# A gated delta rule's triangular inverse: level masks moved from GpSimd ahead of a product to VectorE behind it, and VectorE's dense work reordered around the transposes

## The reference, cut to what matters

```python
kk = jnp.einsum('bhnid,bhnjd->bhnij', k, k)
A = jnp.where(strict, beta[..., :, None] * kk * decay, 0.0)
eye = jnp.eye(C, dtype=F32)
rhs = jnp.concatenate([v * beta[..., None], k * (beta * jnp.exp(gc))[..., None]], axis=-1)
sol = lax.linalg.triangular_solve(A + eye, rhs, left_side=True, lower=True, unit_diagonal=True)
u = sol[..., :dv]
w = sol[..., dv:]
```

## Time and profile before

| | |
|---|---|
| median of three runs | 2222.99 us (2217.79 to 2225.85) |
| the profiled execution: its time / its span | 2220.19 us / 2218.4 us |
| mean granted TensorE clock | 0.987 of full speed |
| busy: TensorE matmul / weight loads | 2136.5 us (96%) / 1758.6 us (79%) |
| busy: VectorE / ScalarE / GpSimd | 1151.9 us (52%) / 762.5 us (34%) / 202.2 us (9%) |
| the four pairs' stretch, 1510 to 1810 us: TensorE / weight loads / VectorE / GpSimd busy | 277.98 / 231.02 / 204.56 / 67.29 us of 300 |
| GpSimd's masks L1580 | 24, in 1510.8 to 1761.5 us |

### The profile page before, as it was taken

One profiled execution on the slowest core, in us unless ns is written; L12 is line 12 of the kernel. 1 busy time (PEld: TensorE's weight loads), 2 busy tenths in 40 slices (PEclk: granted clock), 3 DMA queues, 4 the chain that ended last, 5 costly groups with the idle time before them and its releaser, 6 DMA issues. The chain is left out here.

```text
span 2218.4 us, 33573 instructions
## 1 busy us (share of the span) xinstructions
PE 2136.5 (96%) x13592; PEld 1758.6 (79%) x13592; DVE 1151.9 (52%) x1444; ACT 762.5 (34%) x1047; POOL 202.2 (9%) x137
## 2 busy tenths in 40 slices
PE   7999999997988999999999999998999999999998
PEld 6888888774977888888888888877887778888886
DVE  5444434568557544443444443377667665444422
ACT  4322223245233323322322322253554453322221
POOL 2000011000412000001000001103112210000011
PEclk9999999998999999999999999999999999999999
DMA  4322321320012233332233332221111122333321
GB/s 177 95 95 95 119 96 51 119 66 1 4 42 83 90 101 95 98 112 93 76 96 99 98 116 92 77 87 40 39 43 46 50 66 96 95 95 97 121 91 51
DMA packets 48271, 182.95 MB, mean 82 GB/s; under 512 B 6320, under 2 KB 6576, under 8 KB 48048
## 3 DMA queue, kind: packets, MB, share of 16 engines
q1 hardware_dynamic: 48176, 181.58, 25.6%
HBM read 179.46 MB, written 2.10 MB: 82 GB/s over the span
## 5 line engine op out<-in xcount | busy, mean ns | idle before, releaser
L546 PE MATMUL banks<-H,WS 128*128 128x512 f32 x1840 | 733.0, 398 | 18.4 <-DVE H L1695 8.9
L547 PE MATMUL banks<-H,WS 128*128 128x512 f32 x1840 | 720.7, 392 | 0.0
L548 PE MATMUL banks<-H,WS 128*128 128x512 f32 x1840 | 720.6, 392 | 0.0
L1123 ACT ACTIVATE WS<-RAW 128x1024 fp32r<-128x1024 f32 (+1 forms) x310 | 349.1, 1126 | 995.5 <-PE banks L548 981.9
L1616 DVE TENSOR_TENSOR WS<-RAW,WS 128x1024 fp32r<-128x1024 f32 (+1 forms) x310 | 408.7, 1319 | 217.9 <-ACT WS L1123 217.7
L546 PEld LDWEIGHTS banks<-H,WS 128*128 128x128 f32 x1840 | 347.6, 189 | 97.0 <-DVE WS L1616 11.2
L548 PEld LDWEIGHTS banks<-H,WS 128*128 128x128 f32 x1840 | 347.8, 189 | 73.8
L547 PEld LDWEIGHTS banks<-H,WS 128*128 128x128 f32 x1840 | 347.8, 189 | 71.0 <-issue 1.9
L546 PE MATMUL banks<-A,WS 128*128 128x512 f32 x704 | 273.9, 389 | 0.0
L547 PE MATMUL banks<-A,WS 128*128 128x512 f32 x704 | 273.9, 389 | 0.0
L548 PE MATMUL banks<-A,WS 128*128 128x512 f32 x704 | 273.9, 389 | 0.0
(11 more groups left out here) (352 smaller groups left out, 1777.7 us busy)
## 6 DMA issues: line engine op xcount, KB each, us to landing
RAW<-in_w_gate SPq DMA_DIRECT2D x88, 512.0 KB, 3.6
RAW<-in_w_up SPq DMA_DIRECT2D x88, 512.0 KB, 3.6
RAW<-in_w_down SPq DMA_DIRECT2D x64, 704.0 KB, 4.0
RAW<-in_c_in SPq DMA_DIRECT2D x32, 512.0 KB, 3.6
RAW<-in_ab_in SPq DMA_DIRECT2D x22, 512.0 KB, 3.6
RAW<-in_ab_out SPq DMA_DIRECT2D x8, 512.0 KB, 4.2
RAW<-in_c_out SPq DMA_DIRECT2D x8, 512.0 KB, 3.7
X<-in_x SPq DMA_DIRECT2D x4, 512.0 KB, 6.7
```

Of the source, the lines that this page charges most:

```text
L546: pe.matmul(bank[:, :], WS[:, 0, s, cols], src[0][:, r, :], start=first and j == 0, stop=False)
L547: pe.matmul(bank[:, :], WS[:, 0, s, cols], src[1][:, r, :], start=False, stop=False)
L548: mm = pe.matmul(bank[:, :], WS[:, 1, s, cols], src[0][:, r, :], start=False, stop=last and j == len(rows) - 1)
L1123: act.activation(WS[:, 0, c % SPLIT, 0:cols], RAW[:, c % RING, 0:cols], ACT.Copy).then_inc(hi_ready, 1)
```

## The change

- The constants. The 128-wide pair masks go. New are six masks of 64 columns, `minus1` to `minus32`: -1 on the diagonal and on the entries that belong to the level, 0 elsewhere (for all levels but the first the mask is transposed, since it is laid on the product).
- GpSimd makes C_TM once in a pair, in two steps: the strict triangle of C_TTH, then minus the identity. The masks per level are gone: two instructions instead of six in each pair. For p > 0 the first step waits until the previous pair's last u product has read C_TM.
- VectorE makes C_XT as C_TM times `minus1`, for which it now waits for GpSimd's second step, and C_IU in each level as the product in the bank times the level's mask. The product is now that of the whole triangle minus I, and the mask cuts out the level's entries and turns the signs.
- TensorE waits for C_TM in level 0 only.
- VectorE's two pieces of a level stand ahead of the wait for C_XX and the turn; `query_scaled` stands between the two.
- The key norms of the next pair are issued on TensorE ahead of the solves instead of behind `u21`, and on VectorE behind two of the four pieces.

```diff
 for p in range(HEADS // 2):
-    def pairs(m):
-        pool.tensor_tensor(C_TM[:, :, :], C_TTH[:, :, :], half(f"pair{m}"), ALU.mult).then_inc(c_tm.sem, 1)
-
     pool.wait_ge(*c_tth(4 * p + 4))
-    pairs(1)
-    pool.wait_ge(*c_xt1(p + 1))
-    pairs(2)
+    if p:
+        pool.wait_ge(*c_u_mm(5 * p))
+    pool.tensor_tensor(C_TM[:, :, :], C_TTH[:, :, :], half("strict"), ALU.mult).then_inc(c_tm.sem, 1)
+    pool.wait_ge(*c_tm(2 * p + 1))
+    pool.tensor_tensor(C_TM[:, :, :], C_TM[:, :, :], half("ident"), ALU.subtract).then_inc(c_tm.sem, 1)
     for l in range(1, 5):
         pool.wait_ge(*c_u_mm(5 * p + l))
-        pairs(2 << l)
...
-vec.wait_ge(*c_tm(6 * p + 1))
-vec.tensor_tensor(C_XT[:, :, :], half("ident"), C_TM[:, :, :], ALU.subtract).then_inc(c_xt1.sem, 1)
+vec.wait_ge(*c_tm(2 * p + 2))
+vec.tensor_tensor(C_XT[:, :, :], C_TM[:, :, :], half("minus1"), ALU.mult).then_inc(c_xt1.sem, 1)
...
 for l in range(5):
     vec.wait_ge(*c_u_mm(5 * p + l + 1))
     if l == 0:
-        vec.tensor_tensor(C_IU[:, :, :], half("ident"), halves(u_bank[:, :]), ALU.subtract).then_inc(c_iu.sem, 1)
+        vec.tensor_tensor(C_IU[:, :, :], halves(u_bank[:, :]), half("minus2"), ALU.mult).then_inc(c_iu.sem, 1)
     else:
-        vec.tensor_tensor(by_head(C_IU), IDENT_BY_HEAD, two_banks(2), ALU.subtract).then_inc(c_iu.sem, 1)
+        vec.tensor_tensor(by_head(C_IU), two_banks(2), minus_by_head(2 << l), ALU.mult).then_inc(c_iu.sem, 1)
     if l == 1:
         query_decays()
+    piece()
+    if l in (3, 4):
+        query_scaled(l - 3)
     piece()
     if l < 4:
         vec.wait_ge(*c_xx(5 * p + l + 1))
         turn_crossed()
-    if l in (3, 4):
-        query_scaled(l - 3)
-    piece()
+piece()
+piece()
 if p < 3:
     key_norms(p + 1)
-piece()
-piece()
 piece()
 piece()
```

More of the change, by code:

```diff
@@ L51 @@
 NPARAM = sum(n for _, n in PARAMS.values())
-CONSTS = ["ident", "ones", "ones_half", "pair1", "pair2", "pair4", "pair8", "pair16", "pair32", "causal", "future"]
-HALVES = ["ident", "upper", "strict", "pair1", "pair2", "pair4", "pair8", "pair16", "pair32"]
+CONSTS = ["ident", "ones", "ones_half", "causal", "future"]
+HALVES = ["ident", "upper", "strict", "pair1", "pair2", "pair4", "pair8", "pair16", "pair32",
+          "minus1", "minus2", "minus4", "minus8", "minus16", "minus32"]
 NCONST = len(CONSTS) * P + len(HALVES) * CHUNK + SEQ
@@ L64, in constants @@
     pairs = [(s // (2 * m) == t // (2 * m)) & (s // m % 2 == 0) & (t // m % 2 == 1) for m in (1, 2, 4, 8, 16, 32)]
-    halves = [m[:, :CHUNK] + m[:, CHUNK:] for m in (s == t, same & (s <= t), same & (s < t), *pairs)]
-    mats += pairs
+    halves = [m[:, :CHUNK] + m[:, CHUNK:] for m in (s == t, same & (s <= t), same & (s < t), *pairs, *[-1.0 * (m | (s == t)) for m in (pairs[0], *(m.T for m in pairs[1:]))])]
     mats += [s <= t, np.where(s <= t, 0.0, -30000.0)]
@@ L375, in two_banks, with minus_by_head @@
             return PS[rows, first:first + 2, HALF_BANK * upper:HALF_BANK * (upper + 1)].rearrange("p b (e c) -> p b e c", c=CHUNK)
-        IDENT_BY_HEAD = half("ident").rearrange("p (b e) c -> p b e c", b=2)
+        def minus_by_head(m):
+            return half(f"minus{m}").rearrange("p (b e) c -> p b e c", b=2)
         def by_head(t, rows=slice(0, P), cols=slice(0, CHUNK)):
@@ L959, in core @@
                         for l in range(5):
-                            pe.wait_ge(*c_tm(6 * p + l + 2))
                             if l == 0:
+                                pe.wait_ge(*c_tm(2 * p + 2))
                                 pe.wait_ge(*c_x1(p + 1))
@@ L998, in core @@
                         mm.then_inc(c_u21_mm.sem, 1)
-                        if p < 3:
-                            key_norms(p + 1)
                         slot()
@@ L1007, in core @@
                         slot()
+                        if p < 3:
+                            key_norms(p + 1)
                         pe.wait_ge(*c_xt64(p + 1))
```

## The result

With the change the kernel takes **2207.95 us** (median of five runs, 2207.29 to 2209.81). The kernel before took 2219.89 us beside it (2217.79 to 2225.85, five runs). The ratio is 0.994 with a 95% interval of 0.9929 to 0.9951: some 12 us faster by the medians, where 7.1 were forecast.

A forecast was written before the change was run, and what follows sets the result against it. TensorE, busy in 96% of the span, was taken as the bound, with 18.2 us of waits in the four pairs. Terms -8.3 + 2.0 - 0.8 = -7.1 us gave 2213.1, or 2215.9 us against the median; range 2208 to 2223.5.

The forecast's parts named there:

- C_IU of levels 1 to 4: TensorE's waits for C_IU in those levels: 8.3 of 9.2 us go; 4.6 if VectorE's list decides.
- Rival 2: Levels 1 to 4: VectorE's list stays the bound, half the C_IU waits remain; 2219 to 2222 us; 17%.
- The entry: At each pair's start, two GpSimd steps ahead of C_XT delay level 0: 2.0 us lost, bounds 0 and 5.6.
- One wait fewer ahead of the u products: Weight loads of L968 stand idle 0.05 us less in each of 16 cases: 0.8 us gained.
- Key norms ... I take 0: Moving them between levels and solves gains nothing, as no wait there changes; 1.5 us cost if ScalarE's copy were short.
- with the clock's losses as they are: The sum left the clock's losses in the four head pairs, 6.8 us together, unchanged.
- the small products between the levels and the solves: Place in pair 0 around which the prediction put the clock's largest fall, 3.4 us.
- rival 1: In the pairs, fewer waits make all three falls of the clock go: -13.9 us, 2209.1 us; 25%.
- Rival 3: The clock falls at every pair's entry and behind the levels, by the key norms: +13.3 us, 2236.3 us; 4%.
- The carry to the median: The sum, made against the profiled execution of 2220.19 us, was carried to the median of 2222.99: 2213.1 became 2215.9.
- wrong if the three dips of the clock are gone: Sign in the profile after: the forecast fails if the pairs' three clock falls are gone, or are six.
- the entry might have cost 5.6 us: At level 0, GpSimd keeping the shared port for both scalings in every pair: 5.6 us lost, not 2.0.

The follow-up runs named there:

- order_only: Kernel before with only VectorE's order changed: both pieces of a level ahead of the wait for C_XX and the turn; 2216.58 us.
- norms_order: Kernel before with VectorE's new order and the key norms' move, GpSimd's six masks per pair kept; 2210.73 us, ratio 0.9956.
- norms_only: Kernel before with only the key norms moved, on TensorE ahead of the solves and on VectorE behind two pieces; 2216.10 us, ratio 0.9967.
- masks_order: The whole change without the key norms' move: masks on VectorE and its new order; 2214.53 us, ratio 0.9963.
- norms_mid: The whole change, but TensorE issues the key norms behind the first slot, directly ahead of `xt64`; 2208.34 us, ratio 0.9943.
- vec_norms_back: The whole change with C_TM in one VectorE pass, low part behind level 0's C_IU, and key norms directly behind `u21` again; 2203.83 us.
- low_behind: The whole change with VectorE's low-part piece moved from ahead of level 0's C_IU to directly behind it; 2206.14 us, ratio 0.993.
- three_steps: The whole change plus a third GpSimd pass over C_TM (times a mask of ones) ahead of C_XT; 2216.75 us.

## Why the prediction was wrong

The time forecast, 2215.9 us, is 8 us above the measured one, and 2207.95 lies just below the range. Against its own profiled execution the forecast was 2213.1, and 2207.29 came. Step by step:

- **C_IU of levels 1 to 4: right.** 8.3 of 9.2 us were to go, and 8.7 went. Its parts can be told apart: the order alone takes 5.0, the masks alone 2.8, and both together 8.7, as the two reasons given (a full list, and GpSimd beside it) would have it. Rival 2, a list of 4.2 us that stays the bound, fell: one wait of 0.5 us is left, in pair 3. The prediction had put 0.3 us of wait in each of three pairs at level 4.
- **The entry: the sign right, the size too large.** +2.0 us was written down and +0.9 came. Pair 3's two waits were to grow by 1.4 us from 0.67; they are 0.92 and 0.41, so they grew by half of that. Pairs 1 and 2 went from 1.13 + 1.67 to 1.90 + 1.42, 0.5 us each where 0.2 was written down. Pair 0 went from 2.65 to 1.90: its clock falls there, TensorE takes longer over its slot, and level 0's C_IU is no longer late. So the sum of waits is small only because a fall of 1.7 us took the place of a wait, and this is no luck of one execution: all four profiled kernels with this entry show it. The first half was under-sized: in pair 1 C_XT started 3.28 us behind GpSimd's first step (2.02 before), where 2.9 had been reckoned. The low part took 1.57 us, between the 1.81 of before and the 1.2 of the estimate.
- **One wait fewer ahead of the u products: not borne out.** 0.8 was written down, and the idle time of those weight loads fell by 0.7 (6.4 to 5.7). But `order_only` (5.7), `norms_order` (5.7) and `norms_only` (5.8) keep the wait and have the same. The longest of before's, 0.65 us at 1600.74, lies in a fall of the clock; the others' longest are 0.4. No run shows a gain from the missing wait.
- **"Key norms ... I take 0": the step that failed.** It weighed only what waits for what. Alone, this part makes the kernel 6.6 us faster with no wait changed, and the kernel that has all but this part stands 5 to 6.6 us above after. With it fails **"with the clock's losses as they are"**: they went from 6.8 to 1.7 us. Of these 5.1, 3.4 are the fall behind pair 0's levels, which belongs to the key norms. The other 1.7 are the entries: the falls of pairs 1 and 2 are gone (3.4), though their waits grew, and pair 0's is new (1.7). Those two are gone in `order_only`, `norms_only` and `norms_order` as well, with the entry unchanged, so they were before's own execution; that part of the 5.1 is luck. A row for the key norms was there: the 3.4 us fall in pair 0 begins behind L996 and L872 standing together, though pairs 1 and 2 have the same two groups and no fall behind the levels. The prediction named "the small products between the levels and the solves" as its place, and then gave the clock to rival 1, whose reason was fewer waits, though the diff takes just these two groups of products apart. Rival 3 even had the move's sign reversed: it feared the key norms "right ahead of the solves", and in none of the eight kernels that have them there does the clock fall behind the levels.
- **The carry to the median.** 2.8 us were added because before's profiled execution, at a mean clock of 0.987, lay that far below the median of three runs (that of the five here is 2219.89, and that of the larger batches 2221.3 to 2223.0). This distance is itself clock: before's runs go from 0.984 (2223 to 2226 us) to 0.988 and 0.989 (2216 to 2221). The changed kernel's stay at 0.987 to 0.989, and its median is 0.7 above its profiled run. That made 2.1 of the 8.

Together: of the 8 us, 5.1 are the clock in the pairs and 2.1 the carry. The waits gave 1.5 more than forecast (-7.8 against -8.3 + 2.0), and the 0.8 counted for the missing wait did not come. The time is that of rival 1 (2209.1), which had 25%, but its mechanism is not what happened: there the clock was to come back because waits in the levels go. `masks_order` has those waits gone and loses 8.6 us of clock in the pairs, 6.9 of it behind the levels. The signs listed ahead of the result pointed the right way: "wrong if the three dips of the clock are gone" was met; a new one stands at pair 0's entry.

The rule by which the entry might have cost 5.6 us, the port pair held as a lock by whoever issues first (the Trainium skill, SBUF — State Buffer, "Who interferes with whom"), agrees with what the rows show of single instructions: beside GpSimd's L1583 a tap is long (two took 2.45 us, against a median of 0.75 for one), and free of it the SiLU product is 0.69. It did not decide here: in pair 1 the scalings (from 1587.62, 2.06 us) lay beside VectorE's instructions that read a bank, which kept their length (L2068, 1.28 us for two; L2006, 0.68), and only the low part, from 1589.19, came out 0.35 longer than its median.

Still open is why the clock's loss outside the pairs differs between executions of one kernel. No kernel here changed anything there.

## What to carry to other kernels

When groups of small matmuls (few columns, or a part of the array) stand between dense ones, do not price a change of their order at nothing because no wait changes: read the granted clock behind them, in more than one execution, and try a dense slot between two groups. Here that was worth some 6 us at one place; `norms_mid` shows that not every such pair of groups costs anything. When you carry a sum from a profiled execution to a median, look first at what clock the execution and the runs were at, since a change may take away the very falls that make the median lie above it. And when a chain of small steps gates a stage, compare the engines: one pass of VectorE in place of two of GpSimd was worth 5.6 us of the 2208, and moving the piece of dense work in front of the gated step another 3.4.

## What the runs showed that was not expected

- The granted clock falls although TensorE has hardly been idle. In before, 1546.42 to 1550.3 us, it goes without a gap from 16 quarter-array products to 16 single-column products to a slot, and the clock drops to 1.2 GHz in that slot. In `vec_norms_back` it waits for nothing from 1536 us on, and the fall begins within the key norms, from 1544.28. The Trainium skill (TensorE: Matmul & The Clock Gate, "What's actually happening") speaks of how busy the array has been and of an idle or cold state; the trace shows the lower level behind work that its rows count as busy throughout.
- The same kernel loses different amounts. `order_only` has two groups of runs 8 us apart, and `vec_norms_back` five runs over 10.8 us. The Trainium skill (TensorE: Matmul & The Clock Gate, the same section) says that a window which runs free of the kernel makes the number of slow products vary from run to run; the trace agrees in kind, with falls in mid-kernel. The Trainium skill (that section again) puts the cost of such slow products at the start under 1% of a typical span; the falls of these executions sum to 19 to 35 us of some 2200, by the upper figure of the table, and the whole change was worth 0.6%.
- Waits and the clock trade. `low_behind` lost half of its gain to one more fall. In `three_steps` the clock lost 6.8 us more in the pairs than in after, for 2.0 us more of waits, though a slow slot also hid a wait that would else have stood there.
